# Expert rows through a DRAM table: seven of eight MoE experts leave the combine matmuls

## What is computed

```python
for l in range(DEPTH):
    mod = c_act @ w_mod[l] + b_mod[l]
    sh1, sc1, g1, sh2, sc2, g2 = jnp.split(mod, 6, axis=-1)
    h = modulate(rms_norm(x, norm_mix[l]), sh1, sc1)
    y = four_mixers(h @ w_in[l]) @ w_out[l]
    x = x + g1[:, None, :] * y
    h = modulate(rms_norm(x, norm_ffn[l]), sh2, sc2)
    f = swiglu(h, ...) if l % 2 == 0 else moe_ffn(h, ...)
    x = x + g2[:, None, :] * f
return rms_norm(x, norm_final)

def moe_ffn(h, router_w, router_b, w1, w3, w2):
    logits = h @ router_w + router_b
    top_v, top_i = lax.top_k(logits, 2)
    top_w = jax.nn.softmax(top_v, axis=-1)
    combine = sum(one_hot(top_i, 8) * top_w[..., None], axis=-2)
    for e in range(8):
        y = y + combine[..., e:e + 1] * swiglu(h, w1[e], w3[e], w2[e])
    return y
```

## Time and profile before

| what | us |
|---|---|
| time, median of 3 runs (1572.98 to 1574.33) | 1573.01 |
| the profiled execution, its own time | 1574.65 |
| its span in the trace | 1572.9 |
| PE busy | 1544.6 |
| DVE busy | 1310.8 |
| ACT busy | 972.1 |

### The profile page before, as it was taken

How to read it: one execution, slowest core, us unless ns; L and a number is a source line. 1 busy time by engine, 2 the same in 40 slices (tenths; PEclk the granted TensorE clock), 3 DMA queues, 4 the chain that set the end, 5 groups by cost and what they waited for, 6 DMA issues and landing times.

```text
span 1572.9 us, 19303 instructions
## 1 busy us (share of the span) xinstructions
PE 1544.6 (98%) x7851; PEld 1255.5 (80%) x7851; DVE 1310.8 (83%) x1186; ACT 972.1 (62%) x852; POOL 49.9 (3%) x118
## 2 busy tenths in 40 slices
PE   7999999999999989999999999999999999999997
PEld 3886789999888568888888888888888888888885
DVE  5888888888674479989799899889998989999987
ACT  2532434444444357777777777777777787777775
POOL 5300100000000010000000000000000000000000
PEclk9999999999999999999999999999999999999999
DMA  9765888887823169999999999999999999999990
GB/s 349 267 236 193 282 315 324 306 296 268 307 84 131 54 230 363 371 364 350 330 370 345 365 367 360 335 356 354 358 370 371 342 333 370 349 368 372 344 353 30
DMA packets 158182, 481.04 MB, mean 306 GB/s; under 512 B 4234, under 2 KB 8502, under 8 KB 158086
## 3 DMA queue, kind: packets, MB, share of 16 engines
q1 hardware_dynamic: 156160, 475.02, 82.1%
q0 software_dynamic: 1392, 3.58, 0.7%
q10 hardware_dynamic: 534, 1.13, 0.2%
HBM read 478.66 MB, written 1.05 MB: 305 GB/s over the span
## 4 chain that ended last, share of the span: by engine, by line
PE 95%; DVE 2%; DMA 2%; ACT 1%; issue 0%; SPq 0%; DVEq 0%; ACTq 0%
PE bank L1175 20%; PE bank L1176 20%; PE bank L1177 20%; PE bank L868 6%; PE bank L1053 4%; PE bank L1092 3%; PE bank L1094 3%; PE bank L1093 3%; PE bank L865 3%; PE bank L1068 2%; PE bank L1069 2%; DMA ring<-in_w_mod_dram 2%; PE bank L1070 2%; PE bank L1206 2%; PE bank L1146 1%; PE bank L784 1%
## 5 line engine op out<-in xcount | busy, mean ns | idle before, releaser
L1836 DVE TENSOR_TENSOR ring_low<-ring,w_high 128x2048 fp32r<-128x2048 f32 x336 | 768.5, 2293 | 101.3 <-ACT w_high L2267 94.1
L2267 ACT ACTIVATE w_high<-ring 128x2048 fp32r<-128x2048 f32 x336 | 646.2, 1925 | 238.9 <-PE bank L1177 229.7
L1175 PE MATMUL bank<-w_high,x_high 128*128 128x512 f32 x896 | 355.8, 397 | 0.6 <-issue 0.6
L1176 PE MATMUL bank<-ring_low,x_high 128*128 128x512 f32 x896 | 355.5, 397 | 0.0
L1177 PE MATMUL bank<-w_high,x_low 128*128 128x512 f32 x896 | 352.7, 394 | 0.0
L1175 PEld LDWEIGHTS bank<-w_high,x_high 128*128 128x128 f32 x896 | 168.6, 188 | 41.7 <-DVE ring_low L1836 1.7
L1177 PEld LDWEIGHTS bank<-w_high,x_low 128*128 128x128 f32 x896 | 168.2, 188 | 39.1
L1176 PEld LDWEIGHTS bank<-ring_low,x_high 128*128 128x128 f32 x896 | 168.3, 188 | 37.0
L2206 ACT ACTIVATE tmp_r<-ring 128x1024 fp32r<-128x1024 f32 x84 | 89.2, 1064 | 148.0 <-PE bank L1094 86.5
L1175 PE MATMUL bank<-w_high,act_high 128*128 128x512 f32 x448 | 177.5, 396 | 0.3 <-DVE ring_low L1836 0.3
L1176 PE MATMUL bank<-ring_low,act_high 128*128 128x512 f32 x448 | 175.8, 392 | 0.0
(11 more groups left out here) (353 smaller groups left out, 1690.4 us busy)
## 6 DMA issues: line engine op xcount, KB each, us to landing
ring<-in_moe_w_dram SPq DMA_DIRECT2D x168, 2048.0 KB, 7.9
ring<-in_w_mod_dram SPq DMA_DIRECT2D x23, 2048.0 KB, 10.8
ring<-in_ffn_w_dram SPq DMA_DIRECT2D x21, 2048.0 KB, 14.0
ring<-in_w_in_dram SPq DMA_DIRECT2D x7, 2048.0 KB, 18.7
ring<-in_w_out_dram SPq DMA_DIRECT2D x4, 2048.0 KB, 13.4
ring<-in_w_in_dram SPq DMA_DIRECT2D x4, 1024.0 KB, 14.8
ring<-in_w_mod_dram SPq DMA_DIRECT2D x2, 1024.0 KB, 16.0
gate_row<-in_b_mod_dram POOLq DMA_DIRECT2D x4, 512.0 KB, 7.6
```

The lines of the kernel that those rows point to most:

```text
L1175: mm(out_, x_h, w_h, start=first, stop=False)
L1176: mm(out_, x_h, w_l, start=False, stop=False)
L1836: tt_(moe_low(u, m // 2)[:, c], moe_slot(u, m // 2)[:, c], w_high[:, m % HIGHS, :].bitcast(F32), ALU.subtract).then_inc(low_made, 1)
L2267: act(w_high[:, m % HIGHS, :], moe_slot(u, m // 2)[:, c], ACT.Copy).then_inc(high_made, 1)
```

## The change

Three edits. First, the experts 0 to 6 of the first pass no longer go through PE's combine. DVE's `row_gate` writes the gated rows to `act_m` in units 2 and 4 as before, and POOL sends them with an indirect DMA to `expert_rows`, a table in DRAM with a row for each token and choice: row t for a token's first expert, row 256 + t for its second. The row numbers are computed for each pair: PE multiplies `dispatch` with `row_of` (`index_sums`, four small matmuls in the first expert of a pair), DVE turns the sums into integers (`indices`); an unused slot gets a number over the bound and is not written. The table is cleared once from `y_low`. DVE waits in unit 9 until the rows have left `act_m`, which the next product overwrites. In the last expert POOL reads the table back into `x_slots` in two pieces of 1 MB, and DVE adds them to x in units 17, 20, 25 and 28. The last expert keeps its combine, and so does the second pass, which doesn't run here.

Second, the first half chunk of `w_mod` for g1 stands ahead of `w_out` in the list of chunks. Third, the gate row of g2 of layer 1 is made in two halves: columns 0 to 511 between `norm_x` and `norm_h`, columns 512 to 1023 within the first fill of `x_slots`; and PE gets one more matmul whose result nobody reads (`keep_clock`), behind the routing's last matmul.

```diff
+            eng.wait_ge(gather_t.sem, gather_t.at("g3", 0))
+            eng.memset(y_low.bitcast(F32), 0.0).then_inc(s_clear, 1)
+            eng.wait_ge(s_clear, 1)
+            for n in range(2 * TT):
+                eng.dma_start(expert_rows[n * P:(n + 1) * P, :], y_low.bitcast(F32)).then_inc(s_zero, 16)
+            eng.wait_ge(s_zero, 2 * TT * 16)
+            for r in range(NE - 1):
+                g, u = r // PAIR, r % PAIR
+                eng.wait_ge(index_v.sem, index_v.at("i", g))
+                eng.wait_ge(row_v.sem, row_v.at("y1", r))
+                eng.indirect_dma_start(expert_rows[:, :],
+                                       bass.IndirectOffsetOnAxis(index[:, g % 2, u * PAIR + u:u * PAIR + u + 1], 0),
+                                       act_m[:, :, :].rearrange("p a n -> p (a n)"), None,
+                                       bounds_check=2 * T + P - 1, oob_is_err=False).then_inc(s_rows_out, 16)
+            eng.wait_ge(s_rows_out, 16 * (NE - 1))
+            eng.wait_ge(fill_v.sem, fill_v.at("l11", NE // PAIR - 1))
+            for n in range(2):
+                if n:
+                    eng.wait_ge(pick_v.sem, pick_v.at("a10"))
+                eng.dma_start(picked, expert_rows[n * T:(n + 1) * T, :].rearrange("(t p) d -> p t d", p=P))\
+                   .then_inc(s_rows_in, 16)
...
         mod_chunk(0, "sc2", 1)
+        mod_chunk(0, "g1", 0)
         wout_chunks(0)
-        mod_chunks(0, "g1")
+        mod_chunk(0, "g1", 1)
...
                 mark(ins.then_inc(route_t.sem, 1), route_t, "most")
+                keep_clock(bank[7], steady, 1)
...
+                    for v in range(PAIR):
+                        e = g * PAIR
+                        for tt in range(TT):
+                            ins = mm(bank[7][:, v * PAIR:(v + 1) * PAIR], dispatch[:, tt, v, :], row_of[:, tt, e:e + PAIR],
+                                     start=tt == 0, stop=tt == TT - 1)
...
-                if not is_first(q, g, u):
+                if q:
                     combine(old)
...
                 turn(0)
-                eng.wait_ge(moe_a.sem, moe_a.at("spread", r))
+                if indexed:
+                    eng.wait_ge(index_v.sem, index_v.at("f", pair(q, g)))
+                if spreads:
+                    eng.wait_ge(spread_a.sem, spread_a.at("s", spread_rep(q, g, u)))
                 turn(1)
...
-                gate(1, 1, (bank[0], bank[1]))
+                done_(stt(out=row_of[:, :, :], in0=sel2, scalar=float(T), in1=token_of[:, 0:TT].unsqueeze(2).to_broadcast([P, TT, NE]),
+                          op0=ALU.mult, op1=ALU.add).then_inc(route_v.sem, 1), "row")
...
+            def row_gate(half, r):
+                eng.wait_ge(unit_used, used_at(r + 1, -1))
+                done(eng, tt_(act_m[:, half, :], bank[4 + half][:, :], gate_row[:, half * W:(half + 1) * W],
+                              ALU.mult).then_inc(row_v.sem, 1), row_v, f"y{half}", r)
...
+            def add_rows(n):
+                if n % 2 == 0:
+                    eng.wait_ge(s_rows_in, 16 * (n // 2 + 1))
+                tt = n % 2
+                done(eng, stt(out=x[:, tt, :], in0=picked[:, tt, :], scalar=route_c[:, 4 + n // 2, tt, 0:1], in1=x[:, tt, :],
+                              op0=ALU.mult, op1=ALU.add).then_inc(pick_v.sem, 1), pick_v, f"a{tt}{n // 2}")
...
-                        if m in (3, 5) and not first:
+                        if m in (3, 5) and q:
                             y_rest((m - 3) // 2, old)
-                        if m == 10 and not first:
+                        if m == 10 and q:
                             sums(old, old_weight, 0)
...
+                        if m == 12 and not q and u == 0:
+                            indices(g)
+                        if m == 9 and not first and not q:
+                            eng.wait_ge(s_rows_out, 16 * r)
+                        if m in (17, 20, 25, 28) and last:
+                            add_rows((17, 20, 25, 28).index(m))
...
                         if m == 14:
+                            if first:
+                                eng.wait_ge(s_zero, 2 * TT * 16)
                             act_lows(0)
...
+                    if q == 0 and part == 0:
+                        gate(1, 1, (bank[0], bank[1]), (1,))
                     fill_low(part, pair(q, 0), 0)
...
                 norm_x(2 * l + 1)
+                if l:
+                    gate(1, 1, (bank[0], bank[1]), (0,))
                 norm_h(2 * l + 1)
```

More of the change, by code:

```diff
@@ L128 @@
 MIX_CONSTS = 26
-N_CONSTS = 85
+N_CONSTS = 86
+UNUSED = 1000.0
 CHAIN = CB * (NC - 1)
@@ L203 @@
         ("lgt lg max0 eq0 cand0 first0 pick0 lg2 max1 eq1 cand1 first1 pick1 sel diff ch1 ch0 one w1 w2 sw1 sw2 wt ch2 "
-         "most most_i idle").split(),
+         "most most_i idle row").split(),
     "route_a":
@@ L225 @@
     "moe_a":
-        ("s0 s1 spread ah0 ah1 s2 s3 ah2 ah3 s4 s5 ah4 ah5 s6 ah6").split(),
+        ("s0 s1 ah0 ah1 s2 s3 ah2 ah3 s4 s5 ah4 ah5 s6 ah6").split(),
     "moe_t":
-        ("spread t0 t1 t2 t3 t4 t5 t6").split(),
+        ("t0 t1 t2 t3 t4 t5 t6").split(),
+    "spread_t":
+        ("s").split(),
+    "spread_a":
+        ("s").split(),
+    "index_t":
+        ("i").split(),
+    "index_v":
+        ("f i").split(),
+    "row_v":
+        ("y0 y1").split(),
+    "pick_v":
+        ("a00 a10 a01 a11").split(),
     "comb_v":
@@ L285, in hybrid_stream_block @@
         scan_keep = sb("scan_keep", [P, T])
+        token_of = sb("token_of", [P, 2 * TT + 1])
         chunk_of = sb("chunk_of", [P, CT_])
@@ L355, in hybrid_stream_block @@
         logits_t = mb("logits_t", [NE, T])
+        row_of = mb("row_of", [P, TT, NE], F32R)
+        index_f = mb("index_f", [P, 2 * PAIR])
+        index = mb("index", [P, 2, 2 * PAIR], I32)
         most = mb("most", [P, 4])
@@ L549, in expert, with combined, spread_rep @@
             return q * NE + g * PAIR + u
-        def combined(r):
-            return r - 1
+        def combined(q, r):
+            return r - NE if q else r - 1
+        def spread_rep(q, g, u):
+            return 1 + g * PAIR + u if q else 0
         def pair(q, g):
@@ L1457, in mod_columns, with gate @@
                          mod_e, "fin", rep)
-            def gate(l, which, b):
+            def gate(l, which, b, halves=(0, 1)):
                 rep = 2 * l + which
@@ L1463, in gate @@
                 eng.wait_ge(gate_t.sem, gate_t.at("sum", rep))
-                for half in range(2):
+                for half in halves:
                     g = gate_row[:, half * W:(half + 1) * W]
@@ L2302, in two_experts @@
                             gated(m - 6)
-                        if m == 13:
-                            eng.wait_ge(moe_t.sem, moe_t.at("spread", r))
-                            done(eng, act(spread[:, :], bank[7][:, 0:T], ACT.Copy).then_inc(moe_a.sem, 1),
-                                 moe_a, "spread", r)
+                        if m == 13 and (q or last):
+                            at = spread_rep(q, g, u)
+                            eng.wait_ge(spread_t.sem, spread_t.at("s", at))
+                            done(eng, act(spread[:, :], bank[7][:, 0:T], ACT.Copy).then_inc(spread_a.sem, 1),
+                                 spread_a, "s", at)
                         if m == 14:
```

50 lines of the change are left out of this document (38 added, 12 removed).

## The result

The changed kernel takes 1557.07 us (median of 4 runs, 1555.43 to 1559.32) against 1572.99 (1572.70 to 1574.33) before: ratio 0.9892, 95% interval 0.9877 to 0.9906. I had forecast 1564.2 and a range of 1559 to 1572: right in sign, but the gain is 15.9 us and not 8.8. The profiled execution has a span of 1555.8 us, 17.1 under that of before.

A forecast was written before the change was run, and what follows sets the result against it. PE was taken to bound the experts, and DVE's queue the stretch from norm_h to the gate. The terms -14.4 + 1.7 + 1.0 + 2.9 + 0 = -8.8 us took 1573.01 to 1564.2 us, range 1559 to 1572.

The forecast's parts named there:

- Combine and spread, off PE: PE in the experts: seven combines go, 12.8 us, and seven times the two spread transposes, 1.6; sum -14.4 us.
- Combine, spread and index sums: PE in the experts: -14.4 us for combines and transposes, +1.7 for 16 index-sum matmuls at one pass each.
- My sign of being right: Distance from one expert's first turn to the next, expected shorter by 1.6 to 2.1 us.
- The scatters: DVE's wait in unit 9: landing taken as 9.4 us, inside a window of 13.0 to 13.5, so no cost.
- Rival B: Scatters land late, DVE waits in unit 9 seven times; no gain from 15.8 us on; chance 0.14.
- The slack of 1.3 us: Behind unit 9's window, before PE needs unit 10's low part: landings up to about 14.5 us cost nothing.
- The clearing and the reading back: Table writes and reads cost nothing; four additions on DVE in the last expert, 5.2 to 6.0 us, add +1.0.
- The divided gate: Ahead of norm_h: DVE waits for the bias' DMA, +5.0 us, less 1.1 and 1.0 regained: +2.9.
- rival C: PE's clock drops before the logits, +2 us, and the last expert adds +2: 1568.2, up to 1570; chance 0.18.
- norm_h starts before 558 us: Ahead of the routing on DVE: a start before 558 us was to show the forecast wrong.
- The chunk of w_mod: g1's first half ahead of w_out in the chunk list: taken as 0, bounds -0.5 to +2 us.
- A: Rival at the gate: it does not wait for its bias; sum -12.7, 1560.3 us; chance 0.10.

The follow-up runs named there:

- e2_no_shift: Changed kernel with token_of in the unused part of eps_col's 32 bytes, so all SBUF tensors stand where they stood before; 1565.65 us, ratio 0.9946.
- e1_pad32: Kernel before with one unused tensor of 32 bytes for each partition behind scan_keep; 1568.91 us, ratio 0.9963.
- e8_scatter_twice: Changed kernel with each expert's rows scattered twice, the second after the first landed, DVE waiting for the second; 1615.72 us, ratio 1.0283.
- e7_gate_only: Kernel before with the last gate divided as in the changed kernel, without the extra keep_clock matmul; 1579.04 us, ratio 1.0037.
- e15_later_scatter: Changed kernel with sixteen idle memsets on GpSimd ahead of each scatter; 1587.87 us, ratio 1.0101.
- e5_both_aligned: Changed kernel with the last gate's first half in the wait for pos and 32 unused bytes behind chosen; 1551.98 us, ratio 0.9857.
- e9_x_odd: Changed kernel, gate's first half in the wait for pos, token_of in eps_col's slot, pads leaving only x_high and x_low 32 bytes off; 1563.75 us, ratio 0.9932.
- e4_gate_pos: Changed kernel with the last gate's first half moved from ahead of norm_h into the routing's wait for pos; 1553.00 us, ratio 0.9867.
- e13_all_128: Changed kernel, gate's first half in the wait for pos, pads putting x_high, x_low, w_high, act_high, act_low at multiples of 128 bytes; 1557.07 us, ratio 0.9888.
- e11: Changed kernel with the gate's first half in the wait for pos and 96 unused bytes behind chosen; 1555.59 us, ratio 0.9865.
- e10: Changed kernel with eight idle memsets on GpSimd ahead of each scatter; 1556.62 us, ratio 0.9893.

## Why the prediction was wrong, point by point

**The step that failed** is the one under "Combine and spread, off PE", and silently under every term of PE's: that with the combine gone the other matmuls keep their step of 0.23 us. I read that step from the earlier trace rows as if it belonged to the matmul's shape. It moved by 0.7 to 1.8% with the place of its operands, on some 4000 matmuls: -5.7 us in the seven distances by e2_no_shift, -4.3 by e1_pad32 in the kernel before. Neither the sum nor a rival had room for it; the range did not either.

**Combine, spread and index sums.** My -14.4 + 1.7 = -12.7 is -12.9 in the seven distances and +0.2 ahead of them; at unmoved addresses (e2_no_shift) these measured -12.9 and +0.3. The index sums are 16 matmuls in the changed kernel, four of them in about 0.45 us, and about one pass each was the right reading of the earlier trace rows. My sign of being right, a distance shorter by 1.6 to 2.1 us, was missed on the far side: 2.4 to 2.9 in the changed kernel.

**The scatters.** 9.4 us by the earlier trace rows was 9.3 (9.2 to 10.7), and that is luck in part: I took it from a load of another kind, and the same scatter landed in 5.7 to 10.4 us when it was issued at other moments. The stall by a DVE instruction, for which I had allowed 2.29 us on top, shows in POOL's times, but inside the 9.3. The window of 13.0 to 13.5 us was 13.0. Rival B did not occur, but I priced it too low. The slack of 1.3 us is 0.7 to 1.1; in working it out I took off the combine and forgot the 0.23 us of the transposes. And behind a long wait PE's clock falls: 58.7 us for 49.6 of DVE's wait in e8_scatter_twice. "No faster than before from 15.8 us on" should have read 15.0 to 15.4 (13.0 + 0.7 or 1.1 + 8.8 / 7) with the clock up, and less with it down.

**The clearing and the reading back** cost nothing visible; the two reads landed after 11.4 us at most. The four additions take 1.28 us each, 5.1 in all, just under my 5.2 to 6.0. My +1.0 for the last expert measured +0.5 at unmoved addresses (100.82 against 100.29) and -0.1 in the changed kernel:

```profile
L1938 DVE SCALAR_TENSOR_TENSOR x<-x_slots,route_c,x 128x1024 f32<-128x1024 f32 x4 | 5.1, 1278 | 0.0
```

**The divided gate.** +2.9 was +3.8 (3.7 to 4.5 in the five further profiles of kernels with the gate at that place and the combine gone). The 5.0 us for norm_h were 5.2 (8.47 us behind the reciprocal, 3.30 before); L1836 came back to 2.29; from the logits to the first expert matmul it was -2.0 where I had 0.8 + 1.0, with the gather at a granted clock of 1.00 and not at 0.50 as in the earlier trace rows. The missing part is the 0.79 us in which DVE waited for the router's matmuls: the piece of rival C that I had left out of the forecast did occur, with a granted clock of 0.59. By the Trainium skill (TensorE: Matmul & The Clock Gate, Part 1) a PE that has had nothing to do for a while goes on at the lower of its two clocks; the rows behind this wait (0.59) and those behind the waits in e7_gate_only and e8_scatter_twice (0.50) agree. Behind PE's waits of 2.0 to 2.6 us in e15_later_scatter the clock fell in two of seven experts. The second half was not quite free either: PE waited 1.0 us for it, where it stood 0.6 at the same place before. My sign "norm_h starts before 558 us" came true, at 557.54, and meant nothing, because all of it began 2.2 us earlier.

**The chunk of w_mod.** 0, and nothing that can be measured. The -2.2 us ahead of the first reciprocal are of the size by which that mark differs between any two profiles; about 1 us of it goes with the addresses.

**The rivals.** A fell with the 5.58 us of wait; B needs a landing that never came; C happened in its first half and was drowned.

## What to carry to other kernels

A small tensor declared early moves all that comes after it, and where matmuls set the time this alone was worth 0.4% (e1_pad32) to 0.8% (e5_both_aligned against e9_x_odd) here: note the step of the untouched matmuls before and after a change, and try a change both with its addresses kept and with them moved before crediting a part with the gain. An instruction that reads a DMA's tile belongs behind the DMA's landing in an in-order queue, and idle time of PE costs more than itself if its clock falls in it. When a window is measured from a trace, the slack behind it deserves an experiment of its own, and its profile has to be read for drops of the clock before the slack is worked out from it.

## What the runs showed of the hardware

- The step of a float32r matmul of 128x128 by 512 columns at full clock lay between 226.7 and 235.1 ns over all layouts. Unused tensors alone took that of act_high with ring_low from 234.3 ns (e4_gate_pos) to 226.7 (e13_all_128). The weight loads took 187 to 189 ns in every layout that was looked at (before, changed, e9, e11, e13).
- A scatter of 128 rows of 4 KB kept POOL for 2.34 us and landed in 9.3 us when issued 0.9 us behind the rows. Issued 4.4 behind them it took 1.43 and landed in 6.2, so at nearly the same moment; issued at 8.3 it took 3.0 and made DVE wait until 16.1 to 16.9 us.
- Those times on POOL follow DVE. In the four profiles (changed, e8, e10, e15) 33 of 35 scatters ended on POOL 0.84 to 0.95 us after the end of the low part that DVE had in work when they began. The other two began 0.04 us behind a low part's start and took 1.0 us; that low part then took 2.37 us, not 2.29. What sets the landing behind POOL's part was not found.
- Behind waits of PE of 3.3 to 7.3 us (changed, e7, e8) its matmuls ran at the lower of its two clock levels, a granted clock of 0.50, for 3 to 6 us more. Behind waits of 2.0 to 2.6 us (e15) this happened twice in seven. The same instructions had such a drop in one profile and none in another (518 to 520 us).
